# A two-layer mixer and expert kernel: attention scores taken for pairs of heads, row sums spread over the expert tiles, and six recurrence levels gathered in one matrix

## The chip, the cores and the metric

The kernel runs on one core of one Trainium2 chip. The metric is the device time in microseconds (us) of one execution, less is better. It is measured in several runs. One more execution is taken with the hardware profiler, and all rows of the trace below come from that one.

## What is computed

The input is 512 tokens of width 1024. After a layer norm there are two layers, each of a mixer and a feed-forward part. The mixer has eight heads of softmax attention with a forget gate ("fox") and four heads of a linear recurrence (HGRN2), the second is a mixture with 16384 experts (PEER). In short:

```python
# mixer: fox attention, 8 heads of 64, causal
c = cumsum(log_f)
s = einsum(q, k) * 64 ** -0.5 + c[query] - c[key]
out = softmax(where(mask, s, -1e30)) @ v
# mixer: HGRN2, 4 heads of 128
o = (q * exp(b)) @ S + A @ v          # b: running sum of log_f in a block
A[t, s] = sum_k q[t] * k[s] * exp(b[t] - b[s])   for s <= t
S = exp(b_last) * S + (k * exp(b_last - b)).T @ v
# feed-forward: the best 16 of 16384 experts for each token and each of 8 heads
act = gelu(u[idx] . x)
ffn = sum((gate * act) * v[idx])
ple = sigmoid(h @ gate_w) * (p @ ple_w)
```

All arithmetic has float32 accuracy. The large products are made from two parts, high and low, in a format that TensorE takes in one pass (`float32r`, three products); small products are plain float32, which TensorE works off in two matmul records for each instruction.

## The kernel before

The program is written engine by engine: one block each for SyncE (DMA queue), TensorE, ScalarE, VectorE and GpSimd. Within a block the order is the order of the lines; between engines there are only semaphores, each wrapped as a `Signal` that counts so many increments in each layer (`pr.mark` increments, `wait_ge` waits). No planner arranges anything: the order below is written out by hand, and it must be the same on all engines.

One layer has these stages. Projections of the normed tokens (`project`, `matmul3`, L582, three products for each), during which VectorE prepares the recurrence's decays. Then the mixer's loop, `for j in range(NH + 1)`, with 17 turns. Then normalisation, the output projection, the router (`queries`, `key_scores`, `key_tops`, `routing`). Then two long stages of 128 tiles of 128 experts each: the product of the tokens 128 to 511 by the tables `u` (with gelu), and the product of the weights by the tables `v`. The first 128 tokens don't go through these tables: their 128 chosen rows of `u` and `v` for each token are fetched by GpSimd with indirect DMAs (`gather_u`, `gather_v`), dotted (`dot`) or added up (`add_row`, L1763) on VectorE.

**The mixer's loop.** Each turn `j` handles two attention tiles `s` and one recurrence tile `j` (head `j // 4`, tokens `j % 4`). An attention tile is 128 queries of one head against their `n = (i + 1) * 128` keys.
- `fox_scores(s)` on TensorE: one float32 product over 64 partitions (L632; a head lies in partitions 0 to 63 or 64 to 127 of `fqT` and `fkT`), two products over 8 partitions that add the low and the high part of the cumulated forget gates (`negc_lo`, `negc_hi`, L636), and a bfloat16 product that adds the causal mask (L638).
- `fox_max(s)` on VectorE (L1459, L1460), `fox_exps(s)` on ScalarE (L923), `fox_turn(s)` on TensorE transposes the probabilities (L646), `fox_copy(s)` on ScalarE takes them from PSUM (L933), `fox_values(s)` multiplies by v (L657), `fox_scaled(s)` on ScalarE divides by the sum (L940), which `fox_sum(s)` on VectorE has inverted. Each of the buffers is double (two score banks, `probs`, `probsT`); the bank of the turned probabilities and that of the outputs are single.
- `level_products(j)` on TensorE makes the matrix A of a recurrence tile in eight levels (L675, L679), of which six blocks are masked. `masked(j)` on VectorE takes them from two banks into two matrices `AT[:, j % 2, g]`, by turns between the two (L1491 the first of each, L1494 the others). `hg_outputs(j)` multiplies both matrices by the values (L705), after the product with the carried state (L701). `decay_turn`, `decay_copy`, `state_update` and `carry` (L690, L950, L714, L1504) carry the state from tile to tile.
- For the next recurrence head, VectorE makes the exponents in turns 0 and 1 of a head (`exponents`, L1419, L1420), ScalarE takes their exponentials at the end of turn 1 (`level_exps`, L906), VectorE multiplies them in turns 2 and 3 (`times_keys_queries`, L1431, L1432).

Attention tiles go head by head: `hd, i = s // NT, s % NT`. The two tiles of a turn are of the same head, with different lengths. On TensorE a turn reads: scores of 2j, level products of j, turn of 2j-1, values of 2j-2, scores of 2j+1, outputs of j-1, turn of 2j, state update of j-1, values of 2j-1.

**The product by the value tables.** For each tile `j`, ScalarE and VectorE split the weights (`w_hi`, `w_lo`, L1746) and the table (`v_hi` L1093, `v_lo` L1753; every second one on GpSimd, L1246). The weights of four tiles are the product of activations and gates, which come back from DRAM scratch by `fetch` on ScalarE's DMA queue (L1098, L1100) and are multiplied in `weights` (L1732). Between them, VectorE adds the rows of the first 128 tokens, `for s in range(ADDED[j - 1], ADDED[j])`. `ADDED` is a list made at the top: none up to tile 6, then one for each tile, and one more at each fourth tile until it is three tiles behind; the remaining four or so are added after the last tile. GpSimd issues three gathers at the start of the stage, then keeps up with `j + 4`, and never runs more than eight buffers ahead.

## Time and profile before

| | us |
|---|---|
| median of 3 runs | 3496.46 |
| lowest and highest run | 3492.28, 3502.75 |
| profiled execution, its own time | 3499.44 |
| its span from first to last instruction | 3497.6 |
| mean granted TensorE clock | 0.977 |

| engine | busy us | share of the span | instructions |
|---|---|---|---|
| TensorE matmul (PE) | 3312.7 | 95% | 17370 |
| TensorE weight load (PEld) | 2930.5 | 84% | 17370 |
| VectorE (DVE) | 2561.4 | 73% | 4637 |
| ScalarE (ACT) | 1385.3 | 40% | 2698 |
| GpSimd (POOL) | 2068.5 | 59% | 1388 |

The shares are means over stages with different limits, so the table alone says nothing about a stage. Matmuls are pipelined: one begins before the one ahead has ended, so what one costs is read from start to start and not from its duration. The granted clock is a share of 2.4 GHz; 0.5 is 1.2 GHz.

### The profile page before, as it was taken

The numbers are of one execution on the slowest core, as the hardware profiler recorded it, in microseconds if no ns is written. First come the engines' busy times: TensorE is split into PE (matmuls) and PEld (weight loads), VectorE is DVE, ScalarE is ACT, GpSimd is POOL, SyncE is SP. The second block draws the span as 40 slices with busy tenths as digits, with TensorE's granted clock in tenths as the row PEclk, the third lists the DMA queues.
The fourth block names the chain that finished last, engine by engine and source line by source line (L and its number), as shares of the span: only waits on it lengthen the run. The fifth ranks groups of instructions, "written<-read, shape, count | busy, mean of one in ns | idle before, by whom it ended". The sixth has DMA issues, their size and how long they took to land. (4 is left out here: it accounts for less than half of the span.)

```text
span 3497.6 us, 47039 instructions
## 1 busy us (share of the span) xinstructions
PE 3312.7 (95%) x17370; PEld 2930.5 (84%) x17370; DVE 2561.4 (73%) x4637; ACT 1385.3 (40%) x2698; POOL 2068.5 (59%) x1388
## 2 busy tenths in 40 slices
PE   5999799899999999999989997998999999999996
PEld 4777589899999978888777766898999998788885
DVE  5945339996876588888867643599868655888888
ACT  1234013366666533333212440133666664333332
POOL 5920576666677655555479025776666776655552
PEclk9999899999999999999989998999999999999998
DMA  3310223588889999999723002255888999999994
GB/s 119 96 55 13 73 85 127 170 296 301 302 326 349 343 363 375 355 355 355 251 72 97 31 25 85 74 171 191 290 299 294 346 350 361 357 364 355 355 353 167
DMA packets 312676, 817.12 MB, mean 234 GB/s; under 512 B 22272, under 2 KB 119552, under 8 KB 309120
## 3 DMA queue, kind: packets, MB, share of 16 engines
q1 hardware_dynamic: 112256, 349.02, 28.9%
q0 software_dynamic: 73728, 268.47, 19.9%
q10 hardware_dynamic: 126464, 196.63, 16.2%
q8 instruction: 139, 2.28, 0.3%
q14 instruction: 89, 0.73, 0.1%
HBM read 712.84 MB, written 101.19 MB: 233 GB/s over the span
## 5 line engine op out<-in xcount | busy, mean ns | idle before, releaser
L1229 POOL TENSOR_TENSOR u_lo<-panel,u_hi 128x1024 fp32r<-128x1024 f32 x256 | 634.2, 2478 | 334.8 <-ACT u_hi L1031 330.9
L582 PE MATMUL ps<-hT_hi,u_lo 128*128 128x384 f32 x2048 | 703.6, 344 | 9.1 <-POOL u_lo L1229 9.1
L582 PE MATMUL ps<-hT_lo,u_hi 128*128 128x384 f32 x2048 | 687.6, 336 | 0.0
L582 PE MATMUL ps<-hT_hi,u_hi 128*128 128x384 f32 x2048 | 687.3, 336 | 0.0
L582 PE MATMUL ps<-v_hi,w_lo 128*128 128x512 f32 x1536 | 600.1, 391 | 13.0 <-DVE w_lo L1746 12.8
L582 PE MATMUL ps<-v_lo,w_hi 128*128 128x512 f32 x1536 | 599.2, 390 | 0.0
L582 PE MATMUL ps<-v_hi,w_hi 128*128 128x512 f32 x1536 | 599.0, 390 | 0.0
L1181 POOL TENSOR_TENSOR ring_hi<-panel,cst 128x512 fp32r<-128x512 f32 x244 | 272.8, 1118 | 503.7 <-PE ps L565 302.3
L1246 POOL TENSOR_TENSOR v_lo<-panel,v_hi 128x1024 fp32r<-128x1024 f32 x128 | 313.9, 2452 | 398.7 <-ACT v_hi L1093 398.6
L1093 ACT CAST v_hi<-panel 128x1024 fp32r<-128x1024 f32 x256 | 269.0, 1052 | 634.0 <-PE ps L582 611.5
L1031 ACT CAST u_hi<-panel 128x1024 fp32r<-128x1024 f32 x256 | 268.1, 1048 | 445.5 <-PE ps L582 441.0
L1746 DVE TENSOR_TENSOR w_lo<-arena,w_hi 128x384 fp32r<-128x384 f32 x256 | 341.4, 1334 | 129.2 <-ACT w_hi L1113 117.6
L1669 DVE TENSOR_TENSOR arena<-ps,arena 128x512 f32<-128x512 f32 x384 | 247.1, 685 | 209.9 <-PE ps L835 202.5
L582 PEld LDWEIGHTS ps<-hT_hi,u_lo 128*128 128x128 f32 x2048 | 387.8, 189 | 9.8 <-POOL u_lo L1229 9.7
L582 PEld LDWEIGHTS ps<-hT_lo,u_hi 128*128 128x128 f32 x2048 | 387.5, 189 | 0.1
L582 PEld LDWEIGHTS ps<-hT_hi,u_hi 128*128 128x128 f32 x2048 | 386.7, 189 | 0.0
L582 PEld LDWEIGHTS ps<-v_hi,w_lo 128*128 128x128 f32 x1536 | 289.3, 188 | 75.2 <-issue 15.3
L1183 POOL TENSOR_TENSOR ring_lo<-panel,ring_hi 128x512 fp32r<-128x512 f32 x244 | 340.3, 1395 | 19.1
L582 PEld LDWEIGHTS ps<-v_hi,w_hi 128*128 128x128 f32 x1536 | 289.4, 188 | 60.3
L582 PEld LDWEIGHTS ps<-v_lo,w_hi 128*128 128x128 f32 x1536 | 289.4, 188 | 60.2
L1763 DVE SCALAR_TENSOR_TENSOR ps<-rows_mem,arena,ps 128x1024 f32<-128x1024 f32 x256 | 327.7, 1280 | 0.7
L1210 POOL DMA_INDIRECT rows_mem<-in_v_rows,arena x256 | 265.5, 1037 | 65.8 <-issue 46.0
(258 smaller groups left out, 5816.2 us busy)
## 6 DMA issues: line engine op xcount, KB each, us to landing
panel<-in_u SPq DMA_DIRECT2D x256, 512.0 KB
panel<-in_v SPq DMA_DIRECT2D x256, 512.0 KB
gate_scratch<-arena ACTq DMA_DIRECT2D x24, 2048.0 KB
act_scratch<-arena ACTq DMA_DIRECT2D x124, 384.0 KB
arena<-act_scratch ACTq DMA_DIRECT2D x62, 768.0 KB
arena<-gate_scratch ACTq DMA_DIRECT2D x62, 768.0 KB
panel<-in_w_in SPq DMA_DIRECT2D x28, 1024.0 KB, 5.2
panel<-in_wq SPq DMA_DIRECT2D x16, 1024.0 KB, 5.0
```

Of the source, the lines that this page charges most:

```text
L582: mm = nc.tensor.matmul(o, lhs[a], rhs[b_], start=(start and n == 0), stop=(stop and n == 2))
L1031: pr.mark(nc.scalar.copy(u_hi[:, j % URING].rearrange("p c n -> p (c n)"), u_tile(j)), u_hi_ready)
L1093: pr.mark(nc.scalar.copy(v_hi[:, j % VRING], v_tile(j)), v_hi_ready)
L1181: nc.gpsimd.tensor_tensor(r_hi[:, at], src, zeros, ALU.subtract).then_inc(ring_hi_ready.sem, 1)
L1183: nc.gpsimd.tensor_tensor(r_lo[:, at], src, r_hi[:, at].bitcast(F32), ALU.subtract).then_inc(ring_lo_ready.sem, 1)
L1210: pr.mark(nc.gpsimd.indirect_dma_start(out=dst, out_offset=None, in_=rows, in_offset=bass.IndirectOffsetOnAxis(ap=idx0[:, s:s + 1], axis=0 ...
L1229: pr.mark(nc.gpsimd.tensor_tensor(u_lo[:, j % URING].rearrange("p c n -> p (c n)"), u_tile(j), u_hi[:, j % URING].rearrange("p c n -> p (c ...
L1246: pr.mark(nc.gpsimd.tensor_tensor(v_lo[:, j % VRING], v_tile(j), v_hi[:, j % VRING].bitcast(F32), ALU.subtract), v_lo_odd)
L1669: last = nc.vector.tensor_tensor(hot[:, k % 2], iota_ps.rearrange("p (o n) -> p o n", o=1) .to_broadcast([P, CHUNK, NK]), places.to_broadc ...
L1746: pr.mark(nc.vector.tensor_tensor(w_lo[:, j % GROUP], wact(j // GROUP)[:, j % GROUP], w_hi[:, j % GROUP].bitcast(F32), ALU.subtract), w_lo ...
L1763: pr.mark(nc.vector.scalar_tensor_tensor(out=acc0, in0=v_rows_in[s % VBUF], scalar=wgt0[:, s:s + 1], in1=acc0, op0=ALU.mult, op1=ALU.add), ...
```

## The change

There are three parts.

**Pairs of heads.** `head_tile(s)` numbers the attention tiles anew: 2j and 2j+1 are now the same token tile of two neighbouring heads, one in partitions 0 to 63 and one in 64 to 127. `fox_scores(j)` makes the scores of both, in pieces of at most 256 columns that alternate between the heads. The low and the high part of the forget gates lie in one tensor of 104 rows, at partitions 0 and 32 and again at 64 and 96, with zeros between, so that one product over 40 partitions takes the place of two over 8. The order of a turn changes on TensorE, ScalarE and VectorE: a tile's probabilities are turned in the turn after that of their scores.

**One matrix.** The six masked levels are copied into one matrix, one after the other, and there is one product by the values.

**Row sums.** `ADDED` rises evenly from tile 6 to the last, and the gathers follow it: none before the loop, then up to one more than `ADDED[j + 5]`.

```diff
-ADDED = [0] * (LATE_DOTS + 1)
-for tile_ in range(LATE_DOTS + 1, NK):
-    ADDED.append(ADDED[-1] + 1 + (tile_ % 4 == 0 and ADDED[-1] < tile_ - 3))
+ADDED = [max(0, (tile_ - LATE_DOTS) * SLOTS // (NK - 1 - LATE_DOTS)) for tile_ in range(NK)]
...
-        negc_hi = sb("negc_hi", [FH, T], F32R)
-        negc_lo = sb("negc_lo", [FH, T], F32R)
-        head_row = sb("head_row", [FH, FH], F32R)
+        negc_parts = sb("negc_parts", [FD + LOW_ROW + FH, T], F32R)
+        negc_hi, negc_lo = ([negc_parts[r:r + FH, :] for r in (at, FD + at)] for at in (0, LOW_ROW))
+        head_row = sb("head_row", [FD + LOW_ROW + FH, FH], F32R)
...
+        def head_tile(s):
+
+            return 2 * (s // (2 * NT)) + s % 2, s // 2 % NT
...
-                def fox_scores(s):
-
-                    hd, i = s // NT, s % NT
+                def fox_scores(j):
+
+                    i = j % NT
                     n = (i + 1) * P
-                    o = fox_s_bank(s)
-                    if s >= 2:
-                        pe.wait_ge(probs_ready.sem, layer * probs_ready.per_layer + s - 1)
-                    rows_ = slice(FD * (hd % 2), FD * (hd % 2) + FD)
-                    nc.tensor.matmul(o[:, 0:n], fqT[rows_, hd // 2, i * P:(i + 1) * P], fkT[rows_, hd // 2, 0:n],
-                                     start=True, stop=False)
-
-                    for part_ in (negc_lo, negc_hi):
-                        nc.tensor.matmul(o[:, 0:n], head_row[:, hd:hd + 1].to_broadcast([FH, P]), part_[:, 0:n],
-                                         start=False, stop=False)
-                    pr.mark(nc.tensor.matmul(o[:, n - P:n], ident_b, cmask_b, start=False, stop=True), scored)
+                    if j >= 1:
+                        pe.wait_ge(probs_ready.sem, layer * probs_ready.per_layer + 2 * j)
+                    pieces = [(0, n)] if n <= 2 * P else [(0, 2 * P), (2 * P, n)]
+                    for k, (c0_, c1_) in enumerate(pieces):
+                        for s in (2 * j, 2 * j + 1):
+                            hd = head_tile(s)[0]
+                            rows_ = slice(FD * (hd % 2), FD * (hd % 2) + FD)
+                            nc.tensor.matmul(fox_s_bank(s)[:, c0_:c1_], fqT[rows_, hd // 2, i * P:(i + 1) * P],
+                                             fkT[rows_, hd // 2, c0_:c1_], start=(k == 0), stop=False)
+                    for s in (2 * j, 2 * j + 1):
+                        o, hd = fox_s_bank(s), head_tile(s)[0]
+                        rows_ = slice(FD * (hd % 2), FD * (hd % 2) + LOW_ROW + FH)
+                        nc.tensor.matmul(o[:, 0:n], head_row[rows_, hd:hd + 1].to_broadcast([LOW_ROW + FH, P]),
+                                         negc_parts[rows_, 0:n], start=False, stop=False)
+                    for s in (2 * j, 2 * j + 1):
+                        o = fox_s_bank(s)
+                        pr.mark(nc.tensor.matmul(o[:, n - P:n], ident_b, cmask_b, start=False, stop=True), scored)
...
-                    for g in range(2):
-                        mm = nc.tensor.matmul(hg_o_bank[:, 0:HD], AT[:, j % 2, g, :], vv,
-                                              start=(g == 0 and i == 0), stop=(g == 1))
-                    pr.mark(mm, o_done)
+                    pr.mark(nc.tensor.matmul(hg_o_bank[:, 0:HD], AT[:, j % 2, 0, :], vv,
+                                             start=(i == 0), stop=True), o_done)
...
                 for j in range(NH + 1):
+                    carried = j >= 1 and (j - 1) % NT < NT - 1
                     if j < NH:
-                        fox_scores(2 * j)
+                        fox_scores(j)
+                    if j >= 1:
+                        fox_turn(2 * j - 2)
+                    if j < NH:
                         if j == 0:
                             pe.wait_ge(v_ready.sem, layer * v_ready.per_layer + 8)
                         level_products(j)
-                    carried = j >= 1 and (j - 1) % NT < NT - 1
                     if j >= 1:
+                        fox_values(2 * j - 2)
                         fox_turn(2 * j - 1)
                     if carried:
                         decay_turn(j - 1)
                     if j >= 1:
-                        fox_values(2 * j - 2)
-                    if j < NH:
-                        fox_scores(2 * j + 1)
-                    if j >= 1:
                         hg_outputs(j - 1)
-                    if j < NH:
-                        fox_turn(2 * j)
+                        fox_values(2 * j - 1)
                     if carried:
                         state_update(j - 1)
-                    if j >= 1:
-                        fox_values(2 * j - 1)
...
                 for j in range(NH + 1):
+                    if j >= 1:
+                        fox_copy(2 * j - 2)
                     if j < NH:
                         fox_exps(2 * j)
                     if j >= 1:
+                        fox_scaled(2 * j - 2)
                         fox_copy(2 * j - 1)
-                        if (j - 1) % NT < NT - 1:
-                            decay_copy(j - 1)
-                        fox_scaled(2 * j - 2)
                     if j < NH:
                         fox_exps(2 * j + 1)
                     if j >= 1:
+                        if (j - 1) % NT < NT - 1:
+                            decay_copy(j - 1)
                         hg_copy(j - 1)
-                    if j < NH:
-                        fox_copy(2 * j)
-                    if j >= 1:
                         fox_scaled(2 * j - 1)
...
-                for s in range(3):
-                    gather_v(s)
-                sent = 3
+                sent = 0
                 for j in range(1, NK):
                     if j + URING < NK:
                         v_lo_part(j + URING)
-                    while sent < min(j + 4, SLOTS, VBUF + (ADDED[j - 2] if j > 1 else 0)):
+                    while sent < min(ADDED[min(j + 5, NK - 1)] + 1, SLOTS, VBUF + (ADDED[j - 2] if j > 1 else 0)):
                         gather_v(sent)
                         sent += 1
...
+            first(nc.vector.memset(negc_parts[:].bitcast(F32), 0.0))
+            first(nc.vector.memset(head_row[:].bitcast(F32), 0.0))
...
-            nc.vector.tensor_copy(head_row[:], ident[0:FH, 0:FH]).then_inc(casts.sem, 1)
+            for r in (LOW_ROW, FD, FD + LOW_ROW):
+                nc.vector.tensor_copy(head_row[r:r + FH, :], ident[0:FH, 0:FH])
+            nc.vector.tensor_copy(head_row[0:FH, :], ident[0:FH, 0:FH]).then_inc(casts.sem, 1)
...
-                step(nc.vector.tensor_copy(negc_hi[:], negc))
-                pr.mark(nc.vector.tensor_tensor(negc_lo[:], negc, negc_hi[:].bitcast(F32), ALU.subtract),
-                        negc_ready)
+                nc.vector.tensor_copy(negc_hi[1], negc)
+                step(nc.vector.tensor_copy(negc_hi[0], negc))
+                for low in negc_lo:
+                    last = nc.vector.tensor_tensor(low, negc, negc_hi[0].bitcast(F32), ALU.subtract)
+                pr.mark(last, negc_ready)
...
-                    for k in range(3):
-                        for g in range(2):
-                            at, got, where = AT[:, j % 2, g, :], level_bank(g)[:, k * P:(k + 1) * P], level_mask[:, 3 * g + k, :]
-                            if k == 0:
-                                pr.mark(nc.vector.tensor_tensor(at, got, where, ALU.mult), at_ready)
-                            else:
-                                dve.wait_ge(at_ready.sem, layer * at_ready.per_layer + MASKED * j + 2 * k + g - 1)
-                                pr.mark(nc.vector.copy_predicated(at, where.bitcast(U32), got), at_ready)
+                    at = AT[:, j % 2, 0, :]
+                    for lev in range(MASKED):
+                        got, where = level_bank(lev // 3)[:, lev % 3 * P:(lev % 3 + 1) * P], level_mask[:, lev, :]
+                        if lev == 0:
+                            pr.mark(nc.vector.tensor_tensor(at, got, where, ALU.mult), at_ready)
+                        else:
+                            dve.wait_ge(at_ready.sem, layer * at_ready.per_layer + MASKED * j + lev)
+                            pr.mark(nc.vector.copy_predicated(at, where.bitcast(U32), got), at_ready)
...
+                        fox_max(2 * j + 1)
                         masked(j)
-                        fox_max(2 * j + 1)
```

`fox_turn`, `fox_values`, `fox_exps`, `fox_copy`, `fox_scaled` and `fox_max` take their head and length from `head_tile(s)` in place of `s // NT` and `s % NT`.

## Rows read from the trace of the kernel before

**Rows 1.** Busy time by stretch: us, then busy us (and records) of each engine, clock, DMA.
```profile
206.20:331.60 125.40, 122.86 (x815) 95.59 (x815) 75.22 (x290) 59.87 (x195) 0.00 (x0) 0.96 0.07 22
1933.90:2057.70 123.80, 121.29 (x815) 94.04 (x815) 75.25 (x290) 59.79 (x196) 0.00 (x0) 0.97 0.07 23
213.00:216.40 3.40, 3.40 (x16) 3.28 (x17) 2.72 (x13) 1.31 (x5) 0.00 (x0) 0.51 0.00 0
...
1270.00:1700.00 430.00, 430.00 (x1899) 356.06 (x1898) 378.05 (x294) 153.94 (x211) 238.40 (x162) 1.00 1.00 363
```

**Rows 2.** Waits in the first layer's mixer loop: total us, times, longest.
```profile
ACT work L923 <- DVE nmax L1460: 69.8, 25, 22.6
```

**Rows 3.** Timeline of VectorE: start, us, instruction, shapes, idle before it.
```profile
11.72 4.84 DVE L1280 BATCH_NORM_STATS2 stat<-h 128x6 f32<-128x512 f32 x8 [0.20 <-DMA lng<-in_emb_b]
...
76.00 1.40 DVE L1375 CAST negc_hi<-work 8x512 fp32r<-8x512 f32 x1
...
3468.49 3.68 DVE L1802 TENSOR_TENSOR h<-h,ps 128x512 f32<-128x512 f32 x6 [1.58 <-PE ps L582]
```

**Rows 4.** Waits from 1238 to 1256 us, and TensorE's in the whole execution.
```profile
DVE arena L1732 <- DMA arena<-gate_scratch: 6.2, 1, 6.2
...
PE ps L582 <- DVE w_lo L1746: 3.7, 1, 3.7
...
PE ps L582 <- DVE w_lo L1746: 12.8, 4, 5.1
```

**Rows 5.** Busy time by stretch at the beginning of the products by the values.
```profile
1243.90:1248.10 4.20, 0.53 (x3) 0.14 (x2) 3.60 (x5) 0.82 (x2) 0.00 (x0) 0.89 0.98 326
1248.10:1255.00 6.90, 6.90 (x19) 5.42 (x19) 6.03 (x5) 2.82 (x4) 2.92 (x1) 0.57 1.03 317
2968.80:2974.50 5.70, 0.56 (x4) 0.17 (x2) 3.59 (x5) 0.82 (x2) 0.00 (x0) 0.98 0.99 338
```

**Rows 6.** DMA queues and issues, 1217 to 1243.9 us: packets, MB, share; us to landing.
```profile
q0 software_dynamic: 1296, 4.72, 44.3%
...
q10 hardware_dynamic: 2242, 2.30, 24.8%
...
rows_mem<-in_v_rows,arena POOLq DMA_INDIRECT x8, 11.4
```

**Rows 7.** Timeline of TensorE in a turn of the mixer loop.
```profile
247.66 1.12 PE L632 MATMUL ps<-arena 64*128 64x512 f32 x2
248.72 0.49 PE L636 MATMUL ps<-negc_lo,head_row 8*128 8x512 f32 x1
...
249.44 0.66 PE L705 MATMUL ps<-arena,rows_mem 128*128 128x128 f32 x4
249.94 0.49 PE L646 MATMUL ps<-cst,work 128*128 128x128 f32 x3
...
250.97 0.49 PE L632 MATMUL ps<-arena 64*128 64x128 f32 x2
...
251.82 0.44 PE L675 MATMUL ps<-arena 128*128 128x128 f32 x2
...
253.85 0.60 PE L646 MATMUL ps<-cst,work 128*128 128x128 f32 x4
```

**Rows 8.** The same, cut off at 252.24 us.
```profile
252.19 0.22 PE L679 MATMUL ps<-rows_mem 128*32 128x32 f32 x2
```

**Rows 9.** Timeline of ScalarE in the mixer loop.
```profile
252.56 1.91 ACT L906 ACTIVATE lng<-lng 128x2048 f32<-128x2048 f32 x1
...
256.18 0.57 ACT L933 COPY work<-ps 128x512 f32<-128x512 f32 x1
...
257.07 0.47 ACT L923 ACTIVATE work<-ps,nmax 128x256 f32<-128x256 f32 x1
```

**Rows 10.** Timeline of VectorE in the mixer loop.
```profile
271.34 0.49 DVE L1491 TENSOR_TENSOR rows_mem<-ps,cst 128x128 f32<-128x128 f32 x2 [1.67 <-PE ps L675]
271.74 0.88 DVE L1494 COPY_PREDICATED rows_mem<-cst,ps 128x128 f32<-128x128 uint32 x4
```

More of the change, by code:

```diff
@@ L50 @@
 MASKED = 6
+LOW_ROW = 32
 STAIR = [TOPK // (a + 1) for a in range(TOPK)]
@@ L644, in fox_turn @@
                         pe.wait_ge(probsT_ready.sem, layer * probsT_ready.per_layer + s)
-                    for j in range(s % NT + 1):
+                    for j in range(head_tile(s)[1] + 1):
                         mm = nc.tensor.transpose(fox_t_bank[:, j * P:(j + 1) * P], probs[:, s % 2, j * P:(j + 1) * P],
@@ L1452, in fox_max @@
                 def fox_max(s):
-                    n = (s % NT + 1) * P
+                    n = (head_tile(s)[1] + 1) * P
                     dve.wait_ge(scored.sem, layer * scored.per_layer + s + 1)
```

10 lines of the change are left out of this document (5 added, 5 removed).

## Prediction, made before the changed kernel was run

> **What bounds the kernel now.** Reading began with the table by stretches. The loop of the mixer (fox attention and HGRN2, `for j in range(NH + 1)`) runs once per layer, 206.2 to 331.6 us and 1933.9 to 2057.7 us: 125.4 and 123.8 us. TensorE is busy for 122.9 and 121.3 of them, VectorE for 75 and ScalarE for 60 [rows 1]. So TensorE's own instruction stream sets the loop, and what others wait for is TensorE: ScalarE's longest wait there, 69.8 us for the maxima, only hands on TensorE's pace [rows 2]. The granted clock is 0.96 and 0.97 in these stretches, and in 213.0 to 216.4 it is 0.51: 1.2 in place of 2.4 GHz [rows 1]. A mean of 0.96 over 125.4 us is 10 us at the lower level, which costs about 5 us; the loop would take 120.3 us without it (second layer 120).
>
> The product by the experts' values (second long stretch, 1270 to 1700) is 430.00 of 430 us of TensorE [rows 1]. Where the row sums matter is its beginning and its end. At the end TensorE is last anyway: VectorE has all 128 rows added and waits another 1.58 us for it [rows 3]. At the beginning TensorE stands: the weights of the third group of tiles wait 6.2 us for a transfer from the gate scratch, and TensorE waits 3.7 us for w_lo in turn; over the whole execution there are four such waits, 12.8 us, the longest 5.1 [rows 4]. Between 1243.9 and 1248.1 it is busy 0.53 of 4.2 us, in the second layer 0.56 of 5.7 us, and after the first of these stands 6.9 us run at a clock of 0.57 [rows 5]. In the 26 us before, the transfer engines are full, and the gathers of value rows take 44.3% of them, 4.72 MB, against 24.8% for the queue that carries the gates; eight are issued, and each takes 11.4 us to land [rows 6].
>
> **The score step.** One `fox_scores` with n=512 runs from 247.66 to 249.44, 1.78 us; with n=128 from 250.97 to 251.82, 0.85 us [rows 7]. That is 0.54 us fixed and 0.31 us for each 128 columns (0.21 for the fp32 product in its two passes, 0.05 for each of the two bias products). The fixed part is three changes of tile shape (64 rows, 8 rows, 128 rows): the product by 512 columns needs 4x512/2.4 GHz, 0.85 us, and the next begins after 1.06, so a change costs 0.2. All four lengths of one head come to 0.85+1.12+1.45+1.78=5.2 us (the middle ones by the same line), two heads to 10.4.
>
> After: a pair of heads changes shape twice in place of six times, and has one bias product per head in place of two. If the halves of the array (partitions 0 to 63 and 64 to 127) work at the same time, a pair costs what one head does: 0.5 fixed and 0.27 per 128 columns, 0.80, 1.02, 1.28, 1.55 for i=0..3, 4.65 for two heads. Whether they overlap no row shows, since before never has two row halves in a row. The nearest row is the small level products: two with different 32-column tiles have both begun by 252.24, with 0.22 us each at 252.19 [rows 8]. That speaks for overlap, and I take it; the other bound is no overlap, 0.27 more per 128 columns, 2.7 us for two heads, 10.7 us of TensorE per layer. The Trainium skill (TensorEngine Tiling, section Tiling Modes) says that changing the tiling mode drains the engine, and that different tiles load and multiply in parallel. The first agrees with the 0.2 us, the second with the row of the small tiles; by it the sum is the one with overlap.
>
> The product by AT is two matmuls of 0.22 each (249.44, four records in 0.5 us [rows 7]); one goes: 16x0.22=3.5 us per layer. In all TensorE's work falls by 4x(10.4-4.65)+4 (fewer entries into another shape, 0.1 each)+3.5, about 30 us per loop, to 87.
>
> **But TensorE then no longer sets the loop; the round trip does.** In the new order everything of a pair hangs on one ring: scores(j), turn(2j-2), level products, values(2j-2), turn(2j-1), then ScalarE's copy and exponential of 2j-1 and 2j+1 (and decay_copy behind them), then values(2j-1) or state_update, then scores(j+1), since scores(j+1) waits for both exponentials of j. Step costs: turn 0.11 per block; level products 251.82 to 253.85, 2.03 us [rows 7]; values 0.22 per block; copy of 512 columns 0.57, exponential of 256 columns 0.47 and 0.1 until its sum is read [rows 9]; a handover TensorE to ScalarE 0.2, back 0.15 (the load of the weights lies bare).
> - i=1: 1.02+0.11+2.03+0.19+0.19+0.16 (scaled)+0.15+0.47+0.27 (decay copy)+0.14+0.22=4.9.
> - i=3: 1.56+0.33+2.03+0.63+0.33+0.19+0.36+0.68+0.27+0.14+0.22=6.7.
> - i=0: over values(2j-1): 0.80+0.44+2.03+0.85+0.44+0.20+0.58+0.14+0.85, and an estimated 0.3 for z of the new head: 6.6.
> - i=2: 5.8 by the same ring. In three heads it begins under the exponentials of the next head's levels, 1.91 us for 2048 of 3584 columns [rows 9], 3.3 in all. They sit before copy(2j-2), where formerly TensorE had a turn's worth of other work in hand; 2.6 us of them come bare: 8.5.
>
> First head 25.4 (it starts empty), the next two 26.7 each, the last 24.1 (no next levels), and the drain 4.8, since turn, copy and values now stand in line twice at the end: 107.7 us against 120.3. The gain is thus 12.6, not 30.
>
> VectorE: the masked levels formerly went to two matrices in turn; the start of one to the next is 0.2 us, 1.3 for six (271.34 to 272.6) [rows 10]. Into one matrix each waits for the one before, 0.29 and 0.03: 1.9 for six, 20 us more in both layers. Its 75 us become 85 of 108, and its turns 5.8 to 6.7, just under the ring's; the ring above includes it. With the old spacing the sum would be 3.3 less.
>
> The clock: TensorE has about 20 us of gaps in each loop, but the work between them is denser. I put three stretches at 1.2 GHz as before, each now partly in gaps, 3.5 us. With that and 1 us for handovers that I have too short, 112 us: 125.4-112=13.4 and 123.8-112=11.8, together **-25**.
>
> **Row sums spread evenly.** The number of additions is the same. Formerly three gathers went out at once and then up to j+4; now one at j=1, then `ADDED[j+5]+1`, so by j=4 four are out in place of eight. The nine that moved in 26 us took 44.3% of the engines, 1.3 us each [rows 6]; four fewer ahead of the gates' transfer bring it in 5.2 us sooner, as much as the longest of TensorE's waits. Of the 12.8 us of waits the 2.3 of the first group of tiles have nothing to do with gathers; 10.5 remain, and the lower clock behind them costs 3 (6.9 us, nearly all at half [rows 5]) and an estimated 1.5 in the second layer. Of 15 I take **-10**: the two long waits and part of the clock. Lower bound nothing, upper 15. The VectorE turns with two additions, one in 17, have 4.2 us against 4.08 of TensorE, with w_lo two tiles ahead, so they cost nothing; without that lead it would be 0.1 us each. The end gains nothing: there were 1.58 us of slack.
>
> **Small edits.** Two memsets ahead of the first norm, with 0.20 us of waiting to hide them [rows 3], about 0.5 bare; three more 8x8 copies before TensorE starts, 0.2 us or less each, since two of 128x128 take 0.49 [rows 10]: **+0.7** together. In each layer one more negc copy and one more subtraction, 1.40 us each [rows 3], go to a VectorE that idles later in the projections; if that slack were gone it would be 2.8 per layer. The moved `head_tile` arithmetic costs nothing on the chip.
>
> **Sum.** 3497.6 span, 3499.4 the profiled execution's own time: -25-10+0.7=-34.5 gives 3464.9. The median of the runs is 3 us below the profiled one: 3462.
>
> **Rivals.**
> - *The row halves do not overlap.* 107.7 becomes 114.5 (of the 10.7 us some lies under waits), with clock 118: 3474. For it: no row with two row halves. Against: the small tiles.
> - *The gates' transfer stays late* since the freed share goes to the v tiles' queue, or the next group stands instead. Then only the loop's 25: 3472. For it: the remaining third of the engines serves the v tiles, which could take more. Against: their demand is fixed by four slots.
> - *Handovers are dearer, or VectorE closes the ring*, with its 20 us more. At 0.8 us more per turn the loops are back where they were, and what is left is the gates' 10: 3487, within 0.3%. For it: eleven handovers hang in a turn, of which before shows only a few in a row. Against: those it shows are short.
> - *Slower: the lower clock takes hold of the loop.* TensorE now pauses in every turn. At 1.2 GHz its 87 us of work become 1.7 times as long (the ratio of the two levels less the bare loads), 61 us more if the whole loop stays low. Half the loop low: 30 us more each, 3516. It decides from 30% of the loop at 1.2 GHz on, where the time passes 3497. For it: 0.96 already, with hardly a gap. Against: the stretches between gaps are denser than before. The Trainium skill (TensorE: Matmul & The Clock Gate, section A second HAM failure mode) speaks for it: short pauses between groups in a cycle through PSUM banks made the clock swing between its levels. The trace agrees so far only in that 10 of 125 us are low.
>
> **How the numbers follow.** Chances: forecast 0.58 (its own range 3450 to 3472), no overlap 0.12, gates still late 0.15, dearer ring 0.10, clock 0.05. 0.3% is 10.5 us, about what a measurement can tell from no change. Faster: the first three, 0.85; same 0.10; slower 0.05. The range goes down to 3443 (overlap, no lower clock, 15 us from the gates, VectorE's chain free) and up to 3484, which takes in both partial rivals together (3484) and half of the dearer ring.
>
> **What would show it.** Loops of 110 to 114 us with TensorE busy below 95 in each; the second product of a score pair starting within 0.05 us of a first one of the other half; the copies of levels 0.32 apart; TensorE waiting for ScalarE's copy at values(2j-1) and longest after the level exponentials; the stands at 1244 and 2969 gone, with five or fewer gathers issued before them. Wrong, if the loops stay above 118 or a clock below 0.9 stands in them.

## The result, and the profile after

The changed kernel took 3467.68 us (median of 4 runs, 3460.42 to 3468.46), the kernel before 3498.45 us beside it: a ratio of 0.9909, 95% interval 0.9888 to 0.993. That is 31 us less, where 34.5 were forecast. The profiled execution took 3467.85 us, with a span of 3466.0. The total came out close to the forecast by luck in part: the mixer loops and the start fell short of their terms, the row sums went over theirs, and the errors nearly cancelled.

Put side by side by stages (from the first to the last instruction of each stage in the two traces), the 31.6 us between the spans are:

| stage | before | after | difference | forecast |
|---|---|---|---|---|
| start to the mixer loop, first layer | 206.2 | 209.6 | +3.4 | +0.7 |
| mixer loop, first layer | 125.4 | 118.8 | -6.6 | -13.4 |
| mixer loop, second layer | 123.8 | 110.5 | -13.3 | -11.8 |
| two products by the values | 530.7, 531.7 | 522.5, 523.4 | -16.5 | -10 |
| all else | 1979.8 | 1981.2 | +1.4 | 0 |

"All else" holds a wait of TensorE for a table of VectorE's in the router of the first layer, 8.5 us in place of 6.1. It was between 5.4 and 8.5 us in the kernels below and was long with the old mixer loop too (8.4 in `rows_only`), so no part of the change is shown to cause it; why it varies stays open.

The loops by stretch (columns as in [rows 1]), then the gap behind the exponentials of the levels, the stretch after it, and the two products by the values:

```profile
209.60:328.40 118.80, 105.70 (x783) 88.93 (x783) 82.09 (x290) 59.68 (x196) 0.00 (x0) 0.89 0.07 23
1925.40:2035.90 110.50, 98.61 (x783) 82.27 (x783) 81.97 (x290) 59.81 (x195) 0.00 (x0) 0.95 0.07 25
222.00:225.00 3.00, 1.51 (x12) 1.25 (x11) 2.84 (x12) 2.59 (x2) 0.00 (x0) 1.00 0.00 0
225.50:232.30 6.80, 6.29 (x28) 5.16 (x29) 3.53 (x12) 3.40 (x13) 0.00 (x0) 0.53 0.01 2
...
1208.30:1730.80 522.50, 522.45 (x2303) 432.15 (x2304) 457.25 (x366) 186.50 (x255) 291.00 (x192) 1.00 0.97 353
2913.00:3436.40 523.40, 522.29 (x2303) 432.24 (x2304) 457.33 (x366) 186.52 (x255) 293.96 (x192) 1.00 0.96 348
```

The granted clock fell from 0.96 and 0.97 to 0.89 and 0.95. A mean of 0.89 over 118.8 us is about 26 us at 1.2 GHz, one of 0.95 over 110.5 about 11; added up from the stretches at 1.2 GHz in the trace, without rounding, it is 27.3 and 10.2 us. Where they stand, TensorE's timeline of the first layer shows:

```profile
223.12 0.39 PE L684 MATMUL ps<-pTs 128*128 128x128 f32 x2
226.01 1.11 PE L666 MATMUL ps<-arena,work 128*128 128x64 f32 x4 [2.50 <-ACT work L937]
...
237.86 0.49 PE L638 MATMUL ps<-arena 64*128 64x128 f32 x4
238.11 0.31 PE L643 MATMUL ps<-negc_parts,head_row 40*128 40x128 f32 x2
238.35 0.28 PE L647 MATMUL ps<-cb 128*128 128x128 bf16 x2
238.47 0.61 PE L655 MATMUL ps<-cst,work 128*128 128x128 f32 x4
```

TensorE stands for 2.50 us until ScalarE copies the turned probabilities, and ScalarE has 3.28 us of exponentials in front of that copy (first line below); the values and turns behind it then run at half the clock (four matmul records of the values in 1.11 us). In the first layer this happens once for each of three heads (stands of 2.50, 2.43 and 2.34 us). In the second the same stand is 2.43 and 2.34 us long for two heads. For the first head it is only 1.05 us: the clock was low from 1936.0 us on, behind a stand of 1.28 us near the beginning of the loop, before any exponentials of levels. The other lines are VectorE's at the start and in the chain of levels:

```profile
222.41 3.28 ACT L910 ACTIVATE rows_mem<-rows_mem 128x2048 f32<-128x2048 f32 x2 [2.09 <-DVE rows_mem L1428]
225.60 0.35 ACT L937 COPY work<-ps 128x256 f32<-128x256 f32 x1
```

```profile
30.67 0.22 DVE L1336 CAST cb<-cst 128x128 bf16<-128x128 f32 x1
30.92 2.32 DVE L1338 CAST head_row<-cst 8x8 fp32r<-8x8 f32 x3
33.25 0.98 DVE L1339 CAST head_row<-cst 8x8 fp32r<-8x8 f32 x1
...
241.63 0.29 DVE L1499 TENSOR_TENSOR rows_mem<-ps,cst 128x128 f32<-128x128 f32 x1 [1.23 <-PE ps L684]
241.95 1.64 DVE L1502 COPY_PREDICATED rows_mem<-cst,ps 128x128 f32<-128x128 uint32 x5
243.50 0.42 DVE L1427 TENSOR_TENSOR lng<-arena 128x256 f32<-128x256 f32 x1
```

TensorE's waits for w_lo in the whole execution, 12.8 us in [rows 4], and then the queues in the 27 us that answer to [rows 6] (1215.9 to 1242.8 us; packets, MB, share of the transfer engines; q0 the gathers, q1 the tiles of v, q10 activations and gates):

```profile
PE ps L585 <- DVE w_lo L1754: 1.1, 1, 1.1
```

```profile
q1 hardware_dynamic: 1086, 3.98, 38.1%
q10 hardware_dynamic: 3254, 3.10, 35.1%
q0 software_dynamic: 901, 3.30, 30.9%
```

The gathers moved 3.30 MB in place of 4.72, and the queue with the gates 3.10 in place of 2.30.

### The profile page after: what moved, and what is told of

The parts are those of the page before. It is cut to its first block and busy times, and to the rows that moved or that the text cites. A ratio compares the mean times of both kernels' runs of the same rounds, so it can differ in the third digit from the quotient of the medians.

```text
span 3466.0 us, 46920 instructions
## 1 busy us (share of the span) xinstructions
PE 3266.3 (94%) x17306; PEld 2907.6 (84%) x17306; DVE 2590.1 (75%) x4646; ACT 1384.5 (40%) x2698; POOL 2070.9 (60%) x1388
## 5 line engine op out<-in xcount | busy, mean ns | idle before, releaser
L1232 POOL TENSOR_TENSOR u_lo<-panel,u_hi 128x1024 fp32r<-128x1024 f32 x256 | 625.5, 2444 | 344.8 <-ACT u_hi L1034 344.5
L1213 POOL DMA_INDIRECT rows_mem<-in_v_rows,arena x256 | 274.2, 1071 | 61.7 <-issue 44.9
```

The lines of the kernel that those rows point to most:

```text
L1213: pr.mark(nc.gpsimd.indirect_dma_start(out=dst, out_offset=None, in_=rows, in_offset=bass.IndirectOffsetOnAxis(ap=idx0[:, s:s + 1], axis=0 ...
L1232: pr.mark(nc.gpsimd.tensor_tensor(u_lo[:, j % URING].rearrange("p c n -> p (c n)"), u_tile(j), u_hi[:, j % URING].rearrange("p c n -> p (c ...
```

## The experiments

The kernel before ran again in each group: 3496.85, 3498.81 and 3497.6 us in the three groups. Kernels of different groups are compared by their ratios to it. Each profile is of one execution.

### 1. Each large part alone

`rows_only` is the kernel before with two edits, `mixer_only` the changed kernel with both undone:

```diff
-ADDED = [0] * (LATE_DOTS + 1)
...
+ADDED = [max(0, (tile_ - LATE_DOTS) * SLOTS // (NK - 1 - LATE_DOTS)) for tile_ in range(NK)]
...
-                for s in range(3):
-                    gather_v(s)
-                sent = 3
+                sent = 0
...
-                    while sent < min(j + 4, SLOTS, ...
+                    while sent < min(ADDED[min(j + 5, NK - 1)] + 1, SLOTS, ...
```

> The kernel before, with only the new list of row sums per tile and the new rule for sending the gathers of value rows; the mixer loop and the setup stay as before. Theory: of the 31 us gained, 16.5 came from here (the two products by the values were 8.2 and 8.3 us shorter). Then the time is 16 to 17 us under the kernel before, both mixer loops stay at 124 to 126 us, TensorE's waits for w_lo fall from 13 us to under 2 us, and no low clock follows the start of either product by the values. The forecast's term was 10 us: then 10 under, with some of the waits left. Rival, the shorter product by the values is a consequence of the new mixer loop (other phases of the throttle or of the queues): then 0 to 3 us under.

> The changed kernel with the old list of row sums and the old gathers; the mixer loop and the setup are the new ones. Theory: the parts are independent, so it stands 14 to 16 us under the kernel before (loops 20 less, the start 3.4 more), the stands of TensorE at the beginning of both products by the values are back (5 to 6 us bare, w_lo waits near 13 us) with a low-clock stretch behind. Rival, the parts share a cause: then this one and the one with the new row sums alone add up to clearly less or clearly more than 31 us (by more than 5).

Measured: `rows_only` 3478.55 us, ratio 0.9945 (0.9926 to 0.9964), 19 us by the ratio; `mixer_only` 3482.15 us, 0.9954 (0.9937 to 0.997), 16 us. The sum of 35 is within 5 of the 31 of both together, so nothing speaks for a common cause. In `mixer_only` the waits for w_lo are back as expected (12.5 us, four times). In `rows_only` both products by the values take 522.1 us, and TensorE has no wait for w_lo left. The expectation of its mixer loops failed in one layer:

```profile
205.80:328.00 122.20, 119.67 (x815) 92.45 (x815) 75.09 (x290) 59.82 (x196) 0.00 (x0) 0.99 0.07 23
1925.40:2058.30 132.90, 130.39 (x815) 100.34 (x815) 74.97 (x290) 60.09 (x195) 0.00 (x0) 0.90 0.06 21
2010.00:2014.20 4.20, 3.75 (x31) 3.12 (x31) 3.63 (x13) 2.37 (x9) 0.00 (x0) 1.00 0.00 0
2014.70:2042.00 27.30, 27.30 (x108) 21.13 (x108) 6.00 (x26) 6.59 (x23) 0.00 (x0) 0.50 0.00 1
```

The old loop, with the same instructions as before, took 132.9 us here: 27.3 us in one piece at 1.2 GHz, with TensorE busy through all of it and only 0.45 us of waiting ahead of it. This execution is the slowest of the six (3489.57; the fastest 3475.07). So the loop of the old form took between 122 and 133 us by its clock alone, and low clock doesn't need a gap. (By its sums, 3.4 us at 1.2 GHz in the loop of 122.2 us and 27.3 in that of 132.9, a us at the lower clock cost 0.45 us there.)

### 2. The exponentials in two goes

Changed kernel; ScalarE's part is shown. VectorE now also signals behind the first four levels, and waits for each half by itself:

```diff
-                    if j % NT == 1 and j // NT + 1 < HH:
-                        level_exps(j // NT + 1)
+                    if j % NT in (1, 2) and j // NT + 1 < HH:
+                        level_exps(j // NT + 1, j % NT - 1)
...
-                    for piece in zed_pieces(hd):
+                    for piece in (zed_pieces(hd)[1:] if part_ else zed_pieces(hd)[:1]):
```

> The changed kernel, with ScalarE's exponentials of the next head's levels made in two goes: the first four levels at the end of turn 1, the rest at the end of turn 2, each as soon as its exponents are there, in place of all behind turn 1. Theory (the forecast's 2.6 us per head lie bare since scores and turns wait behind 3.3 us of exponentials, and the low clock of the loop follows these gaps): the gap behind turn 1 shrinks to about 1 us and another of about 1 us may stand behind turn 2; each loop is 3 to 6 us shorter, loop one more (from 119 to 111 to 115) as its 27 us at 1.2 GHz fall to below 15; total 5 to 12 us under the changed kernel. Rival A, the work is conserved: ScalarE's 3.3 us are bare wherever they stand, since ScalarE is in the ring: within 2 us of the changed kernel, clock as before. Rival B, the low clock has nothing to do with the gaps: loops shorter by 3 us at most and loop one still with some 27 us at 1.2 GHz.

Measured: 3439.43 us (3437.94 to 3444.4), ratio 0.9836 (0.9817 to 0.9855): 26 us below the changed kernel by the ratio (28 by the medians), far more than the 5 to 12 expected. Its loops:

```profile
209.50:311.90 102.40, 93.73 (x783) 78.68 (x783) 81.16 (x290) 59.31 (x195) 0.00 (x0) 1.00 0.09 27
1905.10:2008.40 103.30, 95.28 (x783) 79.78 (x783) 81.31 (x290) 59.62 (x195) 0.00 (x0) 0.98 0.08 27
```

The longest stand of TensorE in them is 1.3 us in place of 2.5, and TensorE's waits for ScalarE's copy in the first loop fell from 10.9 us to 3.6. Rivals A and B both fall. The loops are 16.4 and 7.2 us shorter. How much of it is the gap and how much the clock can be estimated from six loops with the ring of the changed kernel (its own, and those of `mixer_only` and `early_start`), by the sums of the stretches at 1.2 GHz: with 10.2 us of them, 110.5 twice; with 13.7, 113.4; with 23.9, 115.8 twice; with 27.3, 118.8. A line through them rises by 0.42 us per us at the lower clock and meets zero at 106.6; no loop lies more than 1.2 us off it. So, by this estimate, the bare exponentials cost about 106.6-102.4=4 us per loop, and the clock some 12 us in the first layer and 4 in the second.

That the gap brings the low clock is borne out by all the kernels below: in the twelve loops of the six kernels with two goes and the new pairs, each has 0 or 3.4 us at 1.2 GHz; with one go each of the six loops above has 10.2 us or more. The stretch of 3.4 us, where there is one, begins 2.1 us or less behind a stand of 1.1 to 1.3 us near the loop's beginning.

### 3. In one go, but a turn later

```diff
-                    if j % NT == 1 and j // NT + 1 < HH:
+                    if j % NT == 2 and j // NT + 1 < HH:
```

> The changed kernel with the exponentials of the next head's levels in one go as there, but behind turn 2 in place of turn 1. Theory (the gap behind 3.3 us of exponentials in one go is what costs, and the low clock follows it): the gaps of 2.6 to 2.8 us stand one turn later, the low-clock stretches behind them, and loops and total stay as in the changed kernel within 4 us (3464 to 3472). Rival, turn 1 is a bad place and the two goes helped because half of the work left it: 5 to 15 us under the changed kernel.

Measured: 3472.91 us, ratio 0.9929 (0.9915 to 0.9942), 7 us over the changed kernel by the ratio, with intervals that overlap: that it is dearer than the theory's 4 is not shown. The rival, 5 to 15 us under, falls. Loops and timelines (TensorE, then ScalarE):

```profile
209.80:327.60 117.80, 104.86 (x783) 88.39 (x783) 81.60 (x290) 59.21 (x195) 0.00 (x0) 0.88 0.08 23
1922.40:2041.80 119.40, 105.49 (x783) 88.05 (x783) 81.67 (x290) 59.15 (x196) 0.00 (x0) 0.89 0.07 23
```

```profile
232.64 0.33 PE L699 MATMUL ps<-cst,arena 128*128 128x128 f32 x1 [1.49 <-DVE state L1512]
...
234.82 1.54 PE L666 MATMUL ps<-arena,work 128*128 128x64 f32 x6 [1.31 <-ACT work L937]
```

The stand is in two pieces here, 1.49 and 1.31 us with 0.9 us of work between, and the low clock begins between them, in the second or within 1 us behind it, three times in each layer; 27.3 us of each loop run at 1.2 GHz. So the low clock followed the exponentials to the turn where they were put, and came behind a stand in two pieces as behind one in one piece.

### 4. Both products of a pair in one half of the array

```diff
-            return 2 * (s // (2 * NT)) + s % 2, s // 2 % NT
+            return (0, 1, 4, 5)[s // (2 * NT)] + 2 * (s % 2), s // 2 % NT
```

> The changed kernel, with heads paired so that both score products of a pair lie in the same half of the array. Theory: 7 us per loop more at full clock as the forecast had it for its rival without overlap (107.7 to 114.5); what the low clock makes of it is added or taken: loops at 0.89 to 0.95 clock of 118 to 126 us, the total 10 to 18 us over the changed kernel. Rival: under 3 us, as the waits behind the levels' exponentials take it up.

> The kernel with the levels' exponentials in two goes (3439 us), with heads 0 and 2, 1 and 3, 4 and 6, 5 and 7 paired in place of 0 and 1, 2 and 3 and so on, so that both products of a pair lie in the same half of the array (both on partitions 0 to 63, or both on 64 to 127). Same number of instructions, same sizes, same result. Theory (the two halves work at the same time, and the scores lie in what sets the loop): the second product of a pair begins when the first is through, the pair takes 0.27 us more for each 128 columns at full clock, 10.7 us per loop, of which 7 to 10.7 show: 14 to 21 us over the kernel with two goes. Rival A, the halves don't overlap in the changed kernel either: the same time within 2 us. Rival B, they overlap, but the round trip over ScalarE hides it: TensorE busier by 10 us, loops longer by under 3 us each.

Measured: `same_half` 3476.66 us, ratio 0.9943 (0.9924 to 0.9961), 12 us over the changed kernel by the ratio, with intervals that just meet and runs from 3468.88 to 3491.49; its loops are 120.8 (clock 0.93) and 117.2 us (0.96). `split_same_half`, where the clock disturbs less: 3457.77 us, 0.9887 (0.9873 to 0.9901), 18 us over the kernel with two goes; its loops are 109.6 (clock 1.00) and 113.6 us (0.95) against 102.4 and 103.3, and TensorE is busy for 104.4 us of the first, 10.6 more (10.7 by the theory). The theory holds, both its rivals fall. In the second of these loops 10.2 us at 1.2 GHz follow a stand of 1.29 us; the first has the same stand and no low clock. The products of a pair at 128 columns (two products, two records each) in `same_half`:

```profile
238.79 0.71 PE L638 MATMUL ps<-arena 64*128 64x128 f32 x4
239.26 0.41 PE L643 MATMUL ps<-negc_parts,head_row 40*128 40x128 f32 x2
...
239.73 0.61 PE L655 MATMUL ps<-cst,work 128*128 128x128 f32 x4
```

The bias products begin 0.47 us after the first score product, in the changed kernel 0.25 (237.86 to 238.11, above), where the second product of the pair starts 0.01 us after the first. A pair takes 0.94 in place of 0.61.

### 5. The levels in two matrices again

Kernel with two goes, masked levels and products as before the change:

```diff
-                    pr.mark(nc.tensor.matmul(hg_o_bank[:, 0:HD], AT[:, j % 2, 0, :], vv,
-                                             start=(i == 0), stop=True), o_done)
+                    for g in range(2):
+                        mm = nc.tensor.matmul(hg_o_bank[:, 0:HD], AT[:, j % 2, g, :], vv,
+                                              start=(g == 0 and i == 0), stop=(g == 1))
+                    pr.mark(mm, o_done)
```

> The kernel with the levels' exponentials in two goes, with the masked levels put into two matrices in turn and two products by the values, as before the change. VectorE's chain of six is 0.6 us shorter in each of 16 turns, TensorE has one product of 0.22 us more in each. Theory (the ring of TensorE and ScalarE sets a turn, VectorE's masked levels end before it matters): TensorE's 3.5 us per loop show, 5 to 7 us over. Rival, VectorE's turns (81 of 102 us) are what is last: then up to 10 us per loop less, and at least 3 us under; in between, the two cancel and the time is within 2 us.

Measured: 3435.93 us (3434.28 to 3438.12), ratio 0.9823 (0.9811 to 0.9836). The total is 3.5 to 4.5 us lower, about what the two measurements can tell apart; the loops are clearer:

```profile
210.60:308.80 98.20, 94.98 (x815) 81.97 (x815) 73.88 (x290) 59.40 (x195) 0.00 (x0) 1.00 0.08 28
1906.10:2005.50 99.40, 96.19 (x815) 83.17 (x815) 73.84 (x290) 59.40 (x195) 0.00 (x0) 0.98 0.09 28
```

```profile
242.19 0.49 DVE L1501 TENSOR_TENSOR rows_mem<-ps,cst 128x128 f32<-128x128 f32 x2 [0.91 <-PE ps L684]
242.60 0.88 DVE L1504 COPY_PREDICATED rows_mem<-cst,ps 128x128 f32<-128x128 uint32 x4
243.39 0.42 DVE L1430 TENSOR_TENSOR pTs<-arena 128x256 f32<-128x256 f32 x1
```

They are 4.2 and 3.9 us shorter, at the same clock, though TensorE does 16 products more in each. VectorE's six levels take 1.20 us here (242.19 to 243.39) and 1.87 in the changed kernel (241.63 to 243.50). So beside the pairs of heads, and with two goes, this part of the change costs 4 us per layer: the rival's side, at less than half its price. That the profiled total gained less (3436.3 against 3437.0 of span) lies in the other stages: the table wait of 8.4 in place of 5.4 us, 1.8 us more in the second product by the values, and a start 1.1 us later.

### 6. The start

`early_start` moves the memsets to the very start of VectorE's stream and the 8x8 copies ahead of the first norm; `pool_head` (with two goes) gives both to GpSimd:

```diff
+            dve.wait_ge(const_in.sem, 16)
+            for r in (0, LOW_ROW, FD, FD + LOW_ROW):
+                last = nc.vector.tensor_copy(head_row[r:r + FH, :], ident[0:FH, 0:FH])
+            last.then_inc(casts.sem, 1)
             norm(h, first, root0, lambda ins: ins.then_inc(h_ready.sem, 1))
```

```diff
+            nc.gpsimd.memset(negc_parts[:].bitcast(F32), 0.0)
+            nc.gpsimd.memset(head_row[:].bitcast(F32), 0.0).then_inc(head_step.sem, 1)
+            pool.wait_ge(head_step.sem, 1)
             pool.wait_ge(const_in.sem, 16)
+            for r in (0, LOW_ROW, FD, FD + LOW_ROW):
+                nc.gpsimd.tensor_copy(head_row[r:r + FH, :], ident[0:FH, 0:FH]).then_inc(head_step.sem, 1)
```

> The changed kernel, with the two memsets at the very start of VectorE's stream and the four 8x8 copies into the row of heads ahead of the first norm, where GpSimd isn't at work yet. Theory: TensorE's first instruction, at 34.5 us in the changed kernel and 30.6 in the one before, comes back to 31 or earlier, and the total falls by 3 to 4 us; the 8x8 copies take under 0.2 us each there, in place of about 1 us behind the norm, where GpSimd's splits run beside them. Rival: the constants arrive late, so that the wait for them in front of the norm takes back what the copies give: total within 1 us of the changed kernel or above it.

> The kernel with the levels' exponentials in two goes; the two memsets and the four 8x8 copies are made by GpSimd, which waits for nothing but the constants (they land at 13.8 us) and has no other work before 33 us. Theory: the first instruction of TensorE, at 34.5 us in the changed kernel, stands at 30.6 as in the kernel before, and the total is 3.9 us lower, 3435. Rival: the small operations on GpSimd take so long, or disturb VectorE's norm so much, that less than 1 us is left of it.

Measured: `early_start` 3464.44 us, ratio 0.9909 (0.989 to 0.9928), no different from the changed kernel; `pool_head` 3441.32 us, 0.9841 (0.9828 to 0.9854), no different from the one with two goes. VectorE in `early_start`, then GpSimd and TensorE in `pool_head`:

```profile
13.81 0.69 DVE L1334 CAST head_row<-cst 8x8 fp32r<-8x8 f32 x4 [2.22 <-DMA cst<-in_consts]
14.53 4.84 DVE L1281 BATCH_NORM_STATS2 stat<-h 128x6 f32<-128x512 f32 x8
```

```profile
13.94 0.91 POOL L1180 CAST head_row<-cst 8x8 fp32r<-8x8 f32 x4 [12.64 <-DMA cst<-in_consts]
```

```profile
30.64 5.74 PE L570 MATMUL ps<-cst,h 128*128 128x128 f32 x32 [30.64 <-DVE cb L1343]
```

The four copies take 0.69 us while GpSimd is idle, not 3.3; but the norm now waits 2.22 us for the constants, and TensorE starts at 33.3: the rival. On GpSimd the copies disturb nothing, TensorE starts at 30.64 and the loop at 206.0 in place of 209.5. The theory is right about the place; the 3.5 us are not to be seen in the medians. In the profiled execution 2.0 of them went in a longer second product by the values (524.2 us against 522.2), where TensorE waited 1.5 us for w_lo.

### 7. Gathers or additions

Both on the kernel with two goes. `old_gathers` keeps the new list of additions and sends gathers by the old rule; `old_added` has the old list, and sends gathers at the new times:

```diff
+                for s in range(3):
+                    gather_v(s)
+                sent = 3
...
-                    while sent < min(ADDED[min(j + 5, NK - 1)] + 1, SLOTS, ...
+                    while sent < min(j + 4, SLOTS, ...
```

```diff
+ADDED = [0] * (LATE_DOTS + 1)
+for tile_ in range(LATE_DOTS + 1, NK):
+    ADDED.append(ADDED[-1] + 1 + (tile_ % 4 == 0 and ADDED[-1] < tile_ - 3))
```

> The kernel with the levels' exponentials in two goes (3439 us), with the evenly spread row sums kept but the gathers of value rows sent by the old rule: three at once, then up to j + 4. Theory (the gathers ahead of the gates' transfer are the cause of TensorE's stands and of the low clock behind them): the stands of 4 to 6 us at the beginning of both products by the values come back, with the low clock behind, 12 to 17 us over. Rival, the two additions in every fourth of the early tiles were the cause: within 2 us of it, no stands.

> The kernel with the levels' exponentials in two goes, with the gathers sent as in the changed kernel, but VectorE adding the row sums by the old list (one per tile, two in every fourth tile until it has caught up, and none left over at the end). Theory: the list of additions by itself changes nothing, within 2 us. Rival: the tiles with two additions delay w_lo: TensorE waits again, 5 to 15 us over.

Measured: `old_gathers` 3453.33 us, ratio 0.9867 (0.9849 to 0.9884), 11 to 14 us over; `old_added` 3444.3 us, 0.9847 (0.9833 to 0.986), 4 to 5 over with intervals that overlap, and with one wait for w_lo, 0.8 us. Waits for w_lo in all of `old_gathers`, and its stands with what follows the first:

```profile
PE ps L585 <- DVE w_lo L1756: 8.8, 3, 4.4
```

```profile
1226.60:1230.70 4.10, 0.14 (x1) 0.00 (x0) 3.33 (x5) 0.82 (x2) 0.00 (x0) 1.00 1.06 373
1230.90:1237.70 6.80, 6.80 (x23) 5.45 (x24) 5.93 (x5) 3.58 (x5) 2.96 (x1) 0.75 1.07 330
2930.50:2935.10 4.60, 0.21 (x2) 0.08 (x1) 3.57 (x5) 0.82 (x2) 0.00 (x0) 0.97 1.03 336
```

The early gathers alone bring back the stands, a little under the 12 to 17 us expected; the list of additions is worth at most the 4 to 5 us. Its profiled span is 2.1 us longer, 1.7 of them in the second product by the values.

### 8. What helped, together

Two goes, two matrices and the start on GpSimd:

> All that helped together: levels' exponentials in two goes, the masked levels put into two matrices again, memsets and 8x8 copies on GpSimd; row sums, gathers and pairs of heads as in the changed kernel. If the gains add up: 3439 less 3.5 (two matrices) less up to 3.9 (start) gives 3432 to 3436. Rival: the start's gain is lost in what follows it, as the run with it alone had it: 3436.

Measured: 3431.38 us (3429.76 to 3434.0, 5 runs), ratio 0.9809 (0.9795 to 0.9822): 35 us below the changed kernel by the ratio (36 by the medians), 66 below the one before. Its loops:

```profile
207.00:305.20 98.20, 94.98 (x815) 81.97 (x815) 74.00 (x290) 59.40 (x195) 0.00 (x0) 1.00 0.09 28
1902.50:2001.90 99.40, 96.19 (x815) 83.19 (x815) 73.90 (x290) 59.41 (x195) 0.00 (x0) 0.98 0.08 28
```

TensorE is busy for 95 of 98 us: by its busy time it sets the loop again, as before the change, with 25 to 28 us less to do. Beside `split_two_matrices` only the start differs, and this one is 4.5 us faster with intervals that overlap; `pool_head` was 2 us slower than the kernel without its start. So the start's worth lies between nothing and 4 us.

## Why the prediction was right in sum, and where not

**TensorE's share: right in the overlap, wrong in the sum.** The halves of the array overlap (4), 0.27 us per 128 columns as forecast (0.61 us for a pair at 128 columns, 0.88 at 256). The fixed part was taken too large: a pair with 128 columns takes 0.61 us where 0.80 was forecast (237.86 to 238.47). TensorE was busy for 105.7 and 98.6 us, above the 95 of the forecast's test, for the low clock stretches its instructions; in the loop at full clock (2) it is 93.7. That is still 7 us over the 87 of work in the forecast's sum. Part of it is the product by AT: 16 products of 0.22, 3.5 us, were to go, and with them TensorE is busy only 0.9 to 1.3 us longer (5). Where the rest lies stays open; it cost nothing here, since the ring was longer.

**The ring: right, and closer than it deserved.** Forecast 107.7 us at full clock, estimated from the six loops (2) 106.6. The 2.6 us under the exponentials were there (2.50), but taking them out gave back 4 us per loop, not 7.8. VectorE was said to lie just under the ring, with 3.3 us in all for the spacing of the levels. It lies in it: six levels 0.335 apart (forecast 0.32) cost 4 us in each loop (5). So beside the pairs of heads the copy into one matrix is a loss that their gain hid. It was measured on the kernel with two goes; in the changed kernel itself, and alone on the kernel before, it was not run.

**The clock: the step that failed.** The forecast put three stretches at 1.2 GHz as before, 3.5 us; they became some 12 us in the first layer and 4 in the second. The rival with the low clock had the right mechanism: it took hold of 27.3 of 118.8 us, 23% of the loop, under the 30% from which it would have made the kernel slower. The 8 us above the forecast's 3.5 in the first layer stood in no term. By the forecast's own test the loop term was wrong in the first layer (118.8 us at 0.89, where above 118 and below 0.9 counted as wrong). The runs (2, 3) show that most of it comes with the gap behind the exponentials in one go; how long it then stays low (6.8 or 10.2 us in the first layer, 3.4 in the second) they do not explain. The Trainium skill (TensorE: Matmul & The Clock Gate, section A second HAM failure mode) tells of short idle stretches between groups of matmuls, in a kernel that cycles through PSUM banks, that make the clock swing; here the trace agrees, with 2.50 us of stand and a clock of 0.53 behind it. In the forecast I gave its rival 0.05 while three such gaps of 2.6 us per loop stood in my own sum: the two should have been read together.

**The row sums: right cause, too small a size.** Forecast 10, measured 16.5 by stages and 19 by the run alone. The waits for w_lo went from 12.8 to 1.1 us, those of the first group of tiles nearly all included, which were said to have nothing to do with gathers; and all of the low clock behind the stands went with them, 10 us at 1.2 GHz. The gathers are the cause of the stands (7). The forecast's "five or fewer gathers issued before" was not met: seven are issued in those 27 us, and 3.30 MB of them move in place of 4.72. That the end gains nothing was right: in `old_added`, whose list leaves three rows for after the last tile, VectorE's last addition ends 2.6 us later in the first layer's stage than in the kernel with two goes, and the next layer's loop begins as long after the product in both (194 us).

**The small edits: the other miss, 3.4 for 0.7.** The memsets cost 0.6 us (the norm begins at 12.33 in place of 11.72) for 0.5. The 8x8 copies were costed at 0.2 us or less from rows in which GpSimd was idle. Behind the norm GpSimd begins its splits:

```profile
30.83 1.04 POOL L1184 TENSOR_TENSOR ring_hi<-panel,cst 128x512 fp32r<-128x512 f32 x1 [30.38 <-DVE h L1297]
31.95 1.26 POOL L1186 TENSOR_TENSOR ring_lo<-panel,ring_hi 128x512 fp32r<-128x512 f32 x1
33.17 1.04 POOL L1184 TENSOR_TENSOR ring_hi<-panel,cst 128x512 fp32r<-128x512 f32 x1
```

Three of the four copies run beside one of these and end just behind it: they take 0.98, 1.15 and 0.98 us, the last until 34.23 us, with GpSimd's third split at 34.21. The fourth falls between two splits, at 31.91 us, and takes 0.16. The Trainium skill (SBUF — State Buffer, section Who interferes with whom) says that copies and casts of VectorE can contend with GpSimd for a shared pair of ports, and that the later one blocks until the other is through. The trace agrees, with 0.98 us for a copy of 8x8 there and 0.15 in the kernel before, where it began ahead of GpSimd's first split (30.20 and 30.24 us).

**The sum.** Loops 5.3 us short of the forecast, start 2.7 us dearer, all else 1.4: 9.4 lost; row sums 6.5 over it. 31.6 between the spans for 34.5, by errors of opposite sign: that part is luck.

## What to carry to other kernels

When TensorE is relieved and another engine's round trip becomes the bound, look for the longest single piece of work on that trip: it can cost its own stand, and the granted clock after it on top, here about as much again or three times as much. Cut it in pieces and spread it over turns. Judge each part of a change alone against its own chain: one product fewer on TensorE was paid in each turn with 0.67 us more in VectorE's chain, and the total hid it. Ahead of a product that lives on a late transfer, send no earlier than needed what is needed later. A price read from a row holds only while the neighbour on the same memory is in the same state.

## What the runs showed of the hardware that was not expected

- The two row halves of the array worked at once for fp32 products of 64 rows: two products by 128 columns (four records) occupy 0.25 us until the next group starts, 0.47 when both lie in one half.
- In the loop of the old form 27.3 us ran at 1.2 GHz with TensorE busy throughout and 0.45 us of waiting ahead. No gap explains it; what does stays open, and with it why the changed loop had 27.3 us of low clock in one layer and 10.2 in the other, though two of the three gaps are as long in both (2.43 and 2.34 us).
- Each us at the lower clock cost the changed loop about 0.42 us, although TensorE waits for a tenth of it, and the old loop, with hardly a wait, 0.45 (122.2 us with 3.4 us low, 132.9 with 27.3).
- An 8x8 copy on VectorE beside a running GpSimd instruction took about 1 us, until that instruction ended; between two of them it took 0.16.
